# Joining two operands into one matmul in the feed-forward loops of a two-block transformer kernel, with edits to its opening, its first attention and its closing norm

## The reference

```python
# first block
x = x + sliding_window_sink_attention(rms_norm(x, norm_mix), swa_w_in, swa_sinks, swa_w_out)
x = x + swiglu_ffn(rms_norm(x, norm_ffn), w_gate_up, w_down)   # (silu(h @ gate) * (h @ up)) @ down, D_FF = 2816
x = rms_norm(x, final_norm)
# second block, two layers
for layer in range(2):
    x = x + (ab_mixer if layer == 0 else mla_mixer)(rms_norm_2(x, ...), ...)
    hf = rms_norm_2(x, ffn_norm[layer])
    x = x + jnp.square(jax.nn.relu(hf @ ffn_w1[layer])) @ ffn_w2[layer]     # width 4096
return rms_norm_2(x, final_norm)
```

## Time and profile before

| | us |
|---|---|
| runs | 859.71, 860.78, 861.1 (median 860.78) |
| profiled execution | 861.04 |
| its span in the trace | 859.2 |
| TensorE busy | 846.7 |
| VectorE busy | 539.2 |
| ScalarE busy | 432.9 |
| GpSimd busy | 47.3 |
| read from HBM | 147.10 MB |

### The profile page before, as it was taken

One profiled execution on the slowest core, in us unless ns is written; L12 is line 12 of the kernel. 1 busy time (PEld: TensorE's weight loads), 2 busy tenths in 40 slices (PEclk: granted clock), 3 DMA queues, 4 the chain that ended last, 5 costly groups with the idle time before them and its releaser, 6 DMA issues.

```text
span 859.2 us, 13974 instructions
## 1 busy us (share of the span) xinstructions
PE 846.7 (99%) x5674; PEld 763.7 (89%) x5674; DVE 539.2 (63%) x582; ACT 432.9 (50%) x584; POOL 47.3 (6%) x117
## 2 busy tenths in 40 slices
PE   8999999999999999999999999999999999999996
PEld 8877999999998799889999999999868999999995
DVE  5897654444448687986855555567587475555553
ACT  6675533443335686555644444446664454444431
POOL 3100000000000211200000000013000000000000
PEclk9999999999999999999999999999999999999999
DMA  9744355545554574345775555444524385555501
GB/s 335 279 147 149 123 196 195 195 160 188 189 196 151 193 249 147 106 160 168 233 241 175 186 192 191 121 141 148 169 83 149 97 268 182 188 190 180 184 32 50
DMA packets 92183, 148.71 MB, mean 173 GB/s; under 512 B 4497, under 2 KB 71585, under 8 KB 91761
## 3 DMA queue, kind: packets, MB, share of 16 engines
q1 hardware_dynamic: 90608, 143.90, 50.0%
q0 software_dynamic: 1248, 4.02, 1.5%
q10 hardware_dynamic: 288, 0.27, 0.1%
HBM read 147.10 MB, written 1.05 MB: 172 GB/s over the span
## 4 chain that ended last, share of the span: by engine, by line
PE 92%; DVE 3%; ACT 2%; DMA 2%; issue 1%; SPq 1%; DVEq 0%; POOLq 0%; POOL 0%; ACTq 0%
PE bank L1918 29%; PE bank L1919 28%; PE bank L1920 28%; DMA w_raw<-laid_swa_w_in_blocks 2%; ACT arena L1138 1%; PE bank L1990 1%; PE bank L2313 1%; PE bank L2096 1%; PE bank L2115 1%; DVE arena L1852 1%; PE bank L2598 0%; PE bank L2285 0%; PE bank L2132 0%; DVE arena L1361 0%; DVE arena L1866 0%
## 5 line engine op out<-in xcount | busy, mean ns | idle before, releaser
L1192 DVE TENSOR_TENSOR w_lo<-w_raw,w_hi 128x2048 fp32r<-128x2048 f32 (+2 forms) x126 | 282.7, 2251 | 150.6 <-ACT w_hi L681 150.4
L1918 PE MATMUL bank<-xT_hi,w_hi 128*128 128x256 f32 x1068 | 304.9, 286 | 0.3
L1919 PE MATMUL bank<-xT_lo,w_hi 128*128 128x256 f32 x1068 | 302.8, 283 | 0.0
L1920 PE MATMUL bank<-xT_hi,w_lo 128*128 128x256 f32 x1068 | 302.8, 283 | 0.0
L681 ACT ACTIVATE w_hi<-w_raw 128x2048 fp32r<-128x2048 f32 (+1 forms) x128 | 239.5, 1878 | 93.4 <-PE bank L1920 85.6
L1918 PEld LDWEIGHTS bank<-xT_hi,w_hi 128*128 128x128 f32 x1068 | 204.5, 192 | 5.7 <-issue 3.1
L1919 PEld LDWEIGHTS bank<-xT_lo,w_hi 128*128 128x128 f32 x1068 | 204.7, 192 | 2.0 <-issue 0.2
L1920 PEld LDWEIGHTS bank<-xT_hi,w_lo 128*128 128x128 f32 x1068 | 204.6, 192 | 0.2
L1918 PE MATMUL bank<-w_hi,ff_hi 128*128 128x512 f32 x344 | 134.6, 391 | 0.0
L1919 PE MATMUL bank<-w_lo,ff_hi 128*128 128x512 f32 x344 | 134.3, 390 | 0.0
L1920 PE MATMUL bank<-w_hi,ff_lo 128*128 128x512 f32 x344 | 133.9, 389 | 0.0
(11 more groups left out here) (264 smaller groups left out, 724.9 us busy)
## 6 DMA issues: line engine op xcount, KB each, us to landing
w_raw<-in_ffn_w SPq DMA_DIRECT2D x64, 1024.0 KB, 5.3
w_raw<-in_ffn_w_gate_up SPq DMA_DIRECT2D x22, 1024.0 KB, 5.1
w_raw<-in_ab_w_in SPq DMA_DIRECT2D x12, 1024.0 KB, 7.2
w_raw<-in_ffn_w_down SPq DMA_DIRECT2D x11, 1024.0 KB, 5.2
w_raw<-in_swa_w_out SPq DMA_DIRECT2D x4, 1024.0 KB, 7.6
w_raw<-in_ab_w_out SPq DMA_DIRECT2D x4, 1024.0 KB, 4.9
w_raw<-in_c_w_out SPq DMA_DIRECT2D x4, 1024.0 KB, 5.1
w_raw<-laid_swa_w_in_blocks SPq DMA_DIRECT2D x3, 1024.0 KB, 13.5
```

What stands on the lines that cost most here:

```text
L1192: dve.tensor_tensor(view(w_lo, ch), view(w_raw, ch), view(w_hi, ch).bitcast(F32), ALU.subtract).then_inc(S["lo_done"], 1)
L1918: pe.matmul(out, sh, mh, start=first, stop=False)
L1919: pe.matmul(out, sh, ml, start=False, stop=False)
L1920: return pe.matmul(out, sl, mh, start=False, stop=last)
```

## The change

Four edits come together.

1. **Joined operands.** `xT_hi` and `xT_lo` become two views of one tensor `xT`, in which for each of the 8 depth pieces the 256 high columns and the 256 low columns lie side by side. A new helper `feature_stacked` makes one matmul of 512 columns (stationary high weights, moving `[high | low]`) and one of 256 (stationary low weights, moving high) where `feature_major` made three of 256. The 512 columns fill one bank for each of the two pieces of features, so a chunk now writes two banks, and the main sum and the cross term stand apart. A sum over the two (`tensor_reduce`, 1024 PSUM columns to 512 numbers in the new SBUF buffer `ff_g`) is made on VectorE: `gate_sum` and `hidden_of_sum` in the gated loop, `up_sum` in the squared ones. It is used in the gated loop's 8 rounds (gate and up chunk) and for 12 of the 16 up chunks of each squared feed-forward; the first two and the last two groups keep the old form. ScalarE's silu or relu reads `ff_g` and waits for the sum. Before the first joined up chunk of a squared feed-forward TensorE waits until relu has read bank 1.
2. **Opening.** ScalarE's queue issues the first three quarters of the first weights, `gain_cols` goes behind the first quarter of the input on SP's queue, and SP keeps only the last quarter of those weights.
3. **First attention.** The copy of the token factors moves ahead of the low part of the fourth chunk, and the keys are written by one instruction over 128 partitions and two over 64, where four over 64 stood; the scores pick the key heads as `g ^ e` accordingly.
4. **Closing.** The last token tile's second half is finished in two quarters of 256 columns, the last one in bank 2; residual and squares follow in three pieces; the sum of the mean is on VectorE, and the product with the gain is made for the first half before the factor is known.

```diff
+        xT = sb("xT", [P, KT, 2, NT, P], F32R)
+        xT_hi = xT[:, :, 0].rearrange("p k t c -> p t k c")
+        xT_lo = xT[:, :, 1].rearrange("p k t c -> p t k c")
...
+        def main_and_cross(b):
+            return psum[:, b:b + 2].rearrange("p f (s c) -> p f c s", s=2)
...
             for q, done in enumerate((S["head_loaded"], S["head1_loaded"], S["head2_loaded"], loaded[head[0].slot])):
                 sp.dma_start(x_cols[:, k], t_in["x_quarters"][q]).then_inc(S[f"xq{q}_loaded"], 16)
-                if q:
+                if q == 0:
+                    sp.dma_start(gain_cols[:], t_in["norm_mix_cols"]).then_inc(S["gain_cols_loaded"], 16)
+                if q == 3:
                     sp.dma_start(view(w_raw, head[0])[:, k], w[5][:, k]).then_inc(done, 16)
...
-            act.dma_start(gain_cols[:], t_in["norm_mix_cols"]).then_inc(S["gain_cols_loaded"], 16)
-            act.dma_start(view(w_raw, sched["swa_in"][0])[:, 0:2], t_in["swa_w_in_blocks"][5][:, 0:2]).then_inc(S["head_loaded"], 16)
+            for q, done in enumerate((S["head_loaded"], S["head1_loaded"], S["head2_loaded"])):
+                k = slice(2 * q, 2 * q + 2)
+                act.dma_start(view(w_raw, sched["swa_in"][0])[:, k], t_in["swa_w_in_blocks"][5][:, k]).then_inc(done, 16)
...
+            def silu_of_sum(i, it=0):
+                act.wait_ge(S["ff1_gs"], i - 1 + it)
+                act.activation(ff_act[:], ff_g[:], ACT.Silu).then_inc(S["ff1_sg"], 1)
...
-            low_upto(SLOTS)
             dve.wait_ge(S["swa_R_psum"], 1)
             step(dve.tensor_copy(swa_R, bank[2][:, 0:SEQ]))
+            low_upto(SLOTS)
...
+            dve.tensor_tensor(k_dst[:, :, 0, :], k_ps, turned_R, ALU.mult)
+            for here, there in ((slice(0, 64), slice(64, P)), (slice(64, P), slice(0, 64))):
+                last = dve.tensor_tensor(k_dst[there, :, 1, :], k_ps[here], turned_R[here], ALU.mult)
...
+            def gate_sum(ch, i, it=0):
+                dve.wait_ge(S["mm_done"], ch.index + 1 + 3 * it)
+                dve.tensor_reduce(ff_g[:], main_and_cross(0), axis=AX, op=ALU.add).then_inc(S["ff1_gs"], 1)
+
+            def hidden_of_sum(ch, i, it=0, then=None):
+                dve.wait_ge(S["ff1_sg"], i + 1 + it)
+                dve.wait_ge(S["mm_done"], ch.index + 1 + 3 * it)
+                dve.tensor_reduce(ff_g[:], main_and_cross(2), axis=AX, op=ALU.add).then_inc(S["ff1_us"], 1)
+                dve.wait_ge(S["ff1_us"], i - 1 + it)
+                dve.tensor_tensor(ff_h[:], ff_act[:], ff_g[:], ALU.mult).then_inc(S["ff1_h"], 1)
...
             with dve.Fori(0, N1 - 4) as it:
+                gate_sum(c[5], 2, it)
                 low(c[8], it, 3)
                 low(c[9], it, 3)
-                hidden(c[7], 2, it)
+                hidden_of_sum(c[7], 2, it)
                 low(c[10], it, 3)
...
                 with dve.Fori(0, N2 // 2 - 2) as it:
+                    up_sum(f, c[3], 2, it)
                     low(c[6], it, 4)
                     hidden2(f, 2, 0, it)
                     low(c[7], it, 4)
+                    up_sum(f, c[5], 3, it)
...
+            def feature_stacked(ch, b):
+                hi, lo = view(w_hi, ch), view(w_lo, ch)
+                for f in range(2):
+                    for k in range(KT):
+                        pe.matmul(bank[b + f], hi[:, k, f * P:(f + 1) * P], xT[:, k].rearrange("p s t c -> p (s t c)"),
+                                  start=k == 0, stop=False)
+                        last = pe.matmul(bank[b + f][:, 0:SEQ], lo[:, k, f * P:(f + 1) * P],
+                                         xT[:, k, 0].rearrange("p t c -> p (t c)"), start=False, stop=k == KT - 1)
+                last.then_inc(S["mm_done"], 1)
...
             with pe.Fori(0, N1 - 3) as it:
-                gate(c[5], 2, it)
+                arrived(c[5], it, 3)
+                pe.wait_ge(S["ff1_sg"], 2 + it)
+                feature_stacked(c[5], 0)
                 down(c[6], 1, it)
                 arrived(c[7], it, 3)
-                feature_major(c[7], bank[1])
+                feature_stacked(c[7], 2)
...
+                pe.wait_ge(S["ff2_relu"], N2 * f + 2)
+                up2_stacked(c[3], 0)
                 down2(f, c[4], 1, 1)
-                up2(c[5], 1)
-                with pe.Fori(0, N2 // 2 - 2) as it:
+                up2_stacked(c[5], 1)
+                with pe.Fori(0, N2 // 2 - 3) as it:
                     down2(f, c[6], 2, 0, it)
-                    up2(c[7], 0, it)
+                    up2_stacked(c[7], 0, it)
                     down2(f, c[8], 3, 1, it)
-                    up2(c[9], 1, it)
+                    up2_stacked(c[9], 1, it)
...
+                part(c[-2], 0, bank[6][:], HALF_D[0])
+                part(c[-1], 1, bank[6][:], HALF_D[0], end=True).then_inc(S["acc_done"], 1)
+                part(c[-2], 0, bank[7][:], HALF_D[1]).then_inc(S["mm_done"], 1)
+                part(c[-1], 1, bank[7][:, 0:256], LAST_D[1], end=True).then_inc(S["acc_done"], 1)
+                part(c[-1], 1, bank[2][:, 0:256], LAST_D[2], first=True, end=True).then_inc(S["mm_done"], 1)
```

119 lines of the change are left out of this document (86 added, 33 removed).

## The result

The changed kernel takes 855.28 us, the median of 5 runs (855.15 to 857.89), against 861.10 for the kernel before in the same session (5 runs, 859.71 to 861.15). The ratio is 0.9946, with a 95% interval of 0.9934 to 0.9957. The kernel is faster by half a per cent. The forecast was 850.9, 4.4 us too low, and 855.28 lies outside the range of 849.7 to 853.6. The profiled execution took 855.28 us with a span of 853.6 (861.04 and 859.2 before).

A forecast was written before the change was run, and what follows sets the result against it. TensorE's own pace, busy 99% of the span, was taken as the bound. Joined operands 8.5 + attention 0.9 + queues 0.2 + closing 0.3 = 9.9 us off 861.04 gave 851.1, for a median 850.9; range 849.7 to 853.6.

The forecast's parts named there:

- The joined operands, 8.5 us: Feed-forward loops: one matmul fewer in each of 640 pairs saves 13.3 ns a pair, 8.5 us, all on the path.
- the first matmul of 256 columns after one of 512, and the first of 512 after 256, keep their own pace in the rows: TensorE in the loops: changing width costs nothing extra, so a pair takes 227 + 120 = 347 ns.
- the prediction's own sign, a pair above 350 ns: TensorE in the loops: the forecast counts as wrong if a joined pair's pace is over 350 ns.
- The sums and the cover on VectorE: Feed-forward loops: 40 added sums of 1.2 us each stay hidden, with 2.2 us left in the gated loop; cost nothing.
- Rival D: Gated loop: sums over two far columns are slow, at 5 us TensorE waits each round; 863.7 us total, chance 0.05.
- C: Loops: alternating widths keep 360 ns a pair, so only 1.4 us are left; 859.4 us total, chance 0.07.
- The attention, 0.9 us: Before the first scores: earlier copy and three key instructions for four make VectorE ready 1.1 us earlier; TensorE gets 0.9.
- The two queues, +0.2 us: Opening: SP issues one DMA fewer ahead of the fourth chunk's weights; saves 0.2 us, bounds -0.2 and 0.45.
- the gains one later: Opening queues: the first quarter of weights is issued one issue earlier (about 0.45 us), the gains one issue later.
- Rival B: Opening and closing give back their gains because next weights or last store end as now; 852.3 us total, chance 0.14.
- only moves the slack ahead of the fourth chunk: Opening: DMA engines are saturated up to the fourth chunk, so starting the first quarter of weights earlier merely shifts slack.
- The closing, 0.3 us: Last token tile: the first of two last multiplications becomes tensor by scalar, 0.33 to 0.66 us; together 0.3 us saved.

The follow-up runs named there:

- experiment 2: Changed kernel with each joined piece issued as 8 matmuls of 512 columns, then 8 of 256, instead of alternating; 851.99 us, ratio 0.9913 to the kernel before.
- experiment 1: Changed kernel with joined operands alone; opening queues, first attention's entry and closing as in the kernel before; 854.66 us against 859.40, ratio 0.9946.
- experiment 9: Changed kernel with the opening's queues as before the change and 17 instead of 12 small warming matmuls; 853.37 us against 860.82, ratio 0.9916.
- experiment 5: Kernel before with the two-queue edit of the opening alone; 861.02 us against 859.62, ratio 1.0013.
- experiment 10: Changed kernel with the first attention's entry as before the change and 17 instead of 12 warming matmuls; 853.97 us, ratio 0.9931 to the kernel before.
- experiment 6: Kernel before with the re-ordered entry of the first attention alone (copy moved ahead, three key products for four); 860.09 us against 859.62, ratio 0.9997.

## Why the prediction was wrong, by its steps

**The joined operands, 8.5 us: the term that was mis-sized.** The mechanism was right: one matmul fewer for each pair, all of it on the path, and alone it carried the whole gain. The step that failed is "the first matmul of 256 columns after one of 512, and the first of 512 after 256, keep their own pace in the rows". The 227 ns came from six wide matmuls deep in a run (699.81 to 701.17), and the pace of those behind a narrow one was not read. The trace of the kernel before had it: the five from 706.93 take 232 ns each (experiment 2). In the alternation, where every wide matmul follows a narrow one, it is 236, and a pair takes 353 ns, not 347, so 4.6 us came. By the prediction's own sign, a pair above 350 ns, it is wrong. The bounds of the term, nothing and 9.0, held; 8.5 was taken too near the upper one. Grouped by width it gives the 7.9 that were nearly forecast.

The Trainium skill, "TensorE: Matmul & The Clock Gate", section "Back-to-back issue gap", would have 2.5 ns a matmul; an estimated 1.6 us by that. It calls that formula the gap of an isolated matmul, and says that in a stream of weight loads and matmuls both set the spacing. The grouped kernel's 12.4 ns a pair disagree with the 2.5, as the earlier trace rows did, and the section says nothing on alternating widths.

**The sums and the cover on VectorE: right.** A sum took 1.22 to 1.23 us, 1.2 forecast:

```profile
L1751 DVE TENSOR_REDUCE arena<-bank 128x512 f32<-128x1024 f32 x24 | 29.4, 1225 | 88.3 <-PE bank L2023 88.3
```

In the gated loop the low part of the hidden activations is done 2.1 us before its down chunk, 2.2 forecast (the row below ends at 138.22; the chunk starts at 123.54 + 16.79 = 140.33):

```profile
137.53 0.69 DVE L1499 TENSOR_TENSOR ff_lo<-arena,ff_hi 128x512 fp32r<-128x512 f32 x1 [0.70 <-ACT ff_hi L856]
```

No wait for it, or for relu, appears. Rival D is refuted (its 863.7 should read 863.9 by its own sum), and so is C in full: the alternation costs nearly half of what joining saves, not all.

**The attention, 0.9 us: right alone, wrong in the sum.** Experiments 1 and 9 give 1.0 us with the old queues. The step that failed is adding it to the queues' gain. Both edits bring VectorE's low part forward against TensorE's second group, and there was one wait of 0.8 to take (experiments 5 and 10).

**The two queues, +0.2 us: wrong.** The text said "the gains one later" and costed one issue. It was a place behind 256 KB: ScalarE starts 2.1 us later than before, and the first large matmul 0.6 to 0.8. In the changed kernel's trace the longer idle stretch goes with the clock's fall, 1.2 to 1.6 us. Rival B was close in kind: what the opening wins it gives back. But not since a transfer ends at the same time, as B had it; in fact it lost 0.7 us. The cover, that another start of the first quarter "only moves the slack ahead of the fourth chunk", did hold: with the clock full, the queues alone stand 0.3 to 0.6 us ahead at chunk 1 (experiment 5). What the text did not reckon with is what the idle stretch ahead of the first matmul may do to the clock.

**The closing, 0.3 us: right**, 0.27. VectorE's last two multiplications:

```profile
849.96 0.49 DVE L1984 TENSOR_SCALAR x_norm<-x_norm,rstd 128x512 f32<-128x512 f32 x1 [0.66 <-POOL rstd L675]
850.36 0.74 DVE L1985 SCALAR_TENSOR_TENSOR x_norm<-x_res,rstd,gain 128x512 f32<-128x512 f32 x1
```

The product by a scalar takes 0.49 us, in the middle of the bounds 0.33 and 0.66. That it took nothing on the way there holds within 0.1 us.

**The balance.** Forecast 9.9 us; measured in the profiled pair 5.6, of which 1.5 are the fall of the clock in the trace of before that no edit touches. The edits gave 4.6 + 0.27 - 0.74 = 4.1. Of the missing 5.8, 3.9 are the pairs, 1.8 the opening. The text took the whole profiled execution as the base for its sum, without asking if its clock was whole: the three stretches of the earlier trace rows show 1.00, but they leave out 330 to 340 us. That 1.5 us is why the time missed by 4.4 and not by 5.8, and it is luck: nothing in the prediction accounts for it.

## What to carry to other kernels

When a loop's saving hangs on a pace, take the pace from a stretch with the same succession of shapes. Where the trace has none, look at the first few instructions behind a change of shape, keep the range open to the bound, or group the instructions by shape. Two edits that end one wait are worth that wait once. A small transfer that the first instruction needs goes to the head of a queue (2.9 us to landing here, against 4.5). A few more small matmuls ahead of the first large one held up nothing here, and the four kernels that had them kept the clock in the opening; that they are the reason is not shown.

## What the runs showed that was not expected

- Alternating 512 and 256 columns costs TensorE about 5 ns a pair more than groups of eight of each (353 against 348 ns, 3.3 us over 640 pairs). It lies with the wide matmul that follows a narrow one (236 against 227 ns); behind narrow ones the first five wide ones of a run are slow (232 ns each), in the kernel before as well. Writing to another bank each time changed the pair by about 1 ns.
- In four of thirteen traces the clock stood at 1.2 GHz for a little over 3 us of TensorE's full work in the opening. They are the four in which it had idled longest before (1.93 to 2.54 us). In the changed kernel that cost 1.2 to 1.6 us.
- A second fall, for some 3 us between 330 and 345 us, while TensorE shows no idle time, comes in some executions, of the kernel before as well, and costs 1.5 us. It is in eight of the thirteen traces, the three grouped ones among them. In all eight it begins 2.1 to 3.2 us after the start of four matmuls that use 4 of the 128 rows of the array and take 1.98 us together (in the trace of experiment 6 records of the group are missing). Such a group stands in the five other traces too, and the clock stayed. In the first row below, of before, the clock fell at about 336.3, in the second, of after, it stayed:

```profile
333.16 1.98 PE L2285 MATMUL bank<-x_norm,sel 4*128 4x512 f32 x4
```

```profile
332.03 1.98 PE L2373 MATMUL bank<-x_norm,sel 4*128 4x512 f32 x4
```

  No run changed this group, so what brings the fall on stays open. It is the likely reason why runs of one kernel lie in two clusters up to 2 us apart, and so why a median of four tells little below 1 us.
